# Two neighbouring ring slots summed by one set of VectorE instructions, in a hybrid decoder layer

## The chip, the cores and the metric

One core of a Trainium2 chip runs the whole layer as one program. The metric is the device time of that program in microseconds (us); three runs of the kernel before were timed.

## What is computed

One decoder layer on 512 tokens of width 2048, all in float32: an input projection, two token mixers (stick-breaking attention and a gated recurrence), a gated merge, an output projection, and a feed-forward block. The change touches only the up projection of the feed-forward block:

```python
up = rmsnorm(h, g_ffn) @ w_up                 # 2048 -> 2 * 5632
up = causal_depthwise_conv(up, conv_w, conv_b)
gate, val = jnp.split(up, 2, axis=-1)
h = h + (jax.nn.silu(gate) * val) @ w_down    # 5632 -> 2048
```

## The kernel before

**Products in three parts.** Every float32 operand is split into a high part (a copy with fewer bits, made by ScalarE) and a low part (raw minus high, made by VectorE). TensorE does three products for each: high by high, high by low, low by high.

**Seven products for eight.** The up projection multiplies 2x2 blocks of 128x128 weights by 2x2 blocks of activations with seven products (`PRODUCTS`), in the Strassen-Winograd way. A weight slot therefore holds seven blocks of 128 columns: `S4, A12, A22, A11, S1, S3, S2`. Four come from memory; S1 and S3 are sums over two of them, S2 is a sum over S1 and A11, and S4 over A12 and S2. The block in place S4 arrives holding A21.

**The feed-forward stage** is a list of 528 slots, `TABLE`, written out in the program. A group of it has eight "up" slots (one for each pair of 128 rows of the contraction, `kp` 0 to 7, for one tile `f` of 44), followed by "down" slots: none after the first two tiles, two after each of tiles 2 to 5, four after each later one. TensorE does 21 matmuls of 256 columns in an up slot (L2122 to L2124), 12 of 512 columns in a down slot (L2157 to L2159). So a group takes 10 slots for f = 2 to 5 and 12 slots from f = 6 on.

**The ring.** Slot n uses place n % 6 of a ring of six (`w4_raw`, `w4_lo`, `w4_hi`). The low part lies over the raw one; a place takes 7 KB a partition. Places 0 and 1, 2 and 3, 4 and 5 lie next to each other in memory. For slot n:

- SP issues the load (L441) when TensorE has done slot n - 6: `sp_.wait_ge(slot_done, ...)` at L509.
- VectorE makes the block sums of an up slot, `sums(n)` at L1633: three instructions, L1641 (two blocks, 256 columns), L1646 and L1648 (one block each). The second and the third wait by semaphore for the one before.
- ScalarE makes the high part, `hi_slot(n)` at L929 (instruction L937), which for an up slot waits for the count of sums.
- VectorE makes the low part, `lo_slot(n)` at L1650 (instruction L1655), which waits for the high part.
- TensorE waits for the count of low parts in `up_slot(n)` at L2117.

The first 24 slots (`NPRE`) come with their sums made beforehand by DMA; `sums` leaves them out (`summed`). That leaves 328 up slots for which VectorE makes them.

**The order on each engine is written out by hand**, slot by slot, in a function `position(n)` for ScalarE (L1000) and one for VectorE (L1747):

```python
def position(n):        # VectorE
    sums(n + 3)
    lo_slot(n + 2)
    ...                 # then one piece of the conv, combine, normalise, ... work
```

So at position n the queue of VectorE holds sums of slot n + 3, then the low part of slot n + 2, then one of: `combine` (L1685 to L1690), `take_up` (L1697, L1701), `normalise` (L1710, L1713), `conv_tap` (L1725), `product` (L1738), `s_low` (L1744). ScalarE's position n begins with the high part of slot n + 3; behind it come conv terms, SiLU and `take_down` (L996), which copies a finished down bank to a stage buffer. GpSimd then issues a DMA that adds that buffer to the output in memory (L640).

Of the kernel before, what the change touches and what calls it, by code (L numbers as in the profile page):

```python
# [24 lines left out]
ALU = mybir.AluOpType  # L25
ACT = mybir.ActivationFunctionType

P = 128
# [41 lines left out]
RING = 6  # L70
SC = 4 * P
WC = 7 * P
# [39 lines left out]
UPS = [sum(t[0] == "up" for t in TABLE[NPRE:n]) for n in range(SLOTS + 1)]  # L112
# [6 lines left out]
S4, A12, A22, A11, S1, S3, S2 = range(7)  # L119
# [38 lines left out]
def build_program(nc, x_t, wstream, wgates, wslots, wfirst, params, out_t):  # L158
# [7 lines left out]
    def sb(name, cols, at, dt=F32):  # L166
        return nc.alloc_sbuf_tensor_at(name, [P, cols], dt, offset=base + at)
# [70 lines left out]

    K = 1024
    ring_at = [0, 7 * K, 14 * K, 21 * K, R1 + 46 * K, R1 + 53 * K]  # L240
    w4_raw = [sb(f"w4_raw{j}", WC, a) for j, a in enumerate(ring_at)]
    w4_lo = [sb(f"w4_lo{j}", WC, a, F32R) for j, a in enumerate(ring_at)]
    w4_hi = [sb(f"w4_hi{j}", WC, a + 4 * WC, F32R) for j, a in enumerate(ring_at)]
    VC = 7 * HALF
# [89 lines left out]
    w4_in = [sem(f"w4_in{j}") for j in range(RING)]  # L334
    w4_step, w4_sums, w4_hi_ready, w4_ready, slot_done = (
        sem("w4_step"), sem("w4_sums"), sem("w4_hi_ready"), sem("w4_ready"), sem("slot_done"))
# [19 lines left out]
    def place(n):  # L356

        return n, n % RING, n // RING + 1

    def entry(n):  # L360
        return TABLE[n]

    def summed(n):

        return n < NPRE

    def is_up(n):
        return entry(n)[0] == "up"

    def exists(n):  # L370
        return n < SLOTS
# [52 lines left out]
    def blocks(t, j, n=1):  # L424
        return t[:, j * P:(j + n) * P]
# [4 lines left out]
    with nc.Block() as block:  # L430
# [221 lines left out]
        def _(act):  # L652
# [276 lines left out]
            def hi_slot(n):  # L929
                if exists(n):  # L930
                    at_, ring, loads = place(n)
                    if is_up(n) and not summed(n):
                        act.wait_ge(w4_sums, UPS[n] + 1)
                    else:
                        act.wait_ge(w4_in[ring], loads * 16)
                    width = WC if is_up(n) else SC
                    act.activation(w4_hi[ring][:, 0:width], w4_raw[ring][:, 0:width], ACT.Copy).then_inc(w4_hi_ready, 1)  # L937
# [10 lines left out]
            act.wait_ge(unit_done, WSLOTS + START4 - 2)  # L948
            hi_kp(5)
            hi_slot(0)  # L950
            hi_kp(6)
            hi_slot(1)
            tile3(KT - 2)
            hi_slot(2)


# [116 lines left out]
        def _(dve):  # L1073
# [558 lines left out]

            def sums(n):  # L1633

                if not exists(n) or not is_up(n) or summed(n):
                    return
                at_, ring, loads = place(n)
                u = UPS[n]
                w = w4_raw[ring]
                dve.wait_ge(w4_in[ring], loads * 16)  # L1640
                dve.tensor_tensor(blocks(w, S1, 2).rearrange("p (a c) -> p a c", a=2),  # L1641
                                  blocks(w, 0).unsqueeze(1).broadcast_to((P, 2, P)),
                                  blocks(w, A22, 2).rearrange("p (a c) -> p a c", a=2),
                                  ALU.add).then_inc(w4_step, 1)
                dve.wait_ge(w4_step, u * 2 + 1)
                dve.tensor_tensor(blocks(w, S2), blocks(w, S1), blocks(w, A11), ALU.add).then_inc(w4_step, 1)  # L1646
                dve.wait_ge(w4_step, u * 2 + 2)
                dve.tensor_tensor(blocks(w, S4), blocks(w, A12), blocks(w, S2), ALU.add).then_inc(w4_sums, 1)  # L1648

            def lo_slot(n):  # L1650
                if exists(n):
# [15 lines left out]
            split_ahead(START3, KP - 1, 4, 0)  # L1667
            split_ahead(START3, KP - 1, 4, 1)
            sums(0)
            lo_kp(5)  # L1670
            t_sums(6)
            sums(1)
            lo_slot(0)
            lo_kp(6)
            tile3(KT - 2)
            sums(2)
            lo_slot(1)

# [590 lines left out]
```

## Time and profile before

| | |
|---|---|
| Median of 3 runs | 2807.22 us (2806.18 to 2808.89) |
| Span of the profiled execution | 2806.6 us |
| TensorE busy with matmuls | 2798.6 us of it |
| VectorE busy | 2087.2 us |
| ScalarE busy | 1248.4 us |
| GpSimd busy | 428.6 us |
| Feed-forward stage | from about 1438 us to the end |

The profiled execution is one run of the program; its span, from its first to its last instruction, lies 0.6 us under the median of the timed runs. Busy time of one engine can lie beside that of another, and matmuls overlap each other, so the mean time of one matmul is longer than the distance between two starts. In a timeline each row has its start and its duration in us, the engine, the line, the operation and the tiles; what stands in brackets is idle time in front of it and what ended it.

### The profile page before, as it was taken

How to read it: one execution, taken by the hardware profiler on the slowest of the kernel's cores; microseconds unless marked ns; L12 is line 12 of the kernel's file. 1: busy time of each engine (PE TensorE's matmuls, PEld its weight loads, DVE VectorE, ACT ScalarE, POOL GpSimd, SP SyncE). 2: the span in 40 equal slices, each digit the busy share in tenths (PEclk: the TensorE clock that was granted, in tenths of full speed). 3: DMA queues.
4: the chain of work that ended last, by engine and by line, in shares of the span. 5: the costliest groups of instructions: out<-in, count | busy, mean ns of one | idle time of the engine just before them, and what ended most of it. 6: DMA issues, size and time to landing. Idle time of an engine off the chain costs nothing.

```text
span 2806.6 us, 45334 instructions
## 1 busy us (share of the span) xinstructions
PE 2798.6 (100%) x16930; PEld 2513.6 (90%) x16930; DVE 2087.2 (74%) x3913; ACT 1248.4 (44%) x1701; POOL 428.6 (15%) x579
## 2 busy tenths in 40 slices
PE   9999999999999999999999999999999999999999
PEld 7788888888889999888899999999999999999998
DVE  7776677677777777444468987888788878887884
ACT  5444434433334334323355544444444444444543
POOL 1022154324400000001000111111111101110112
PEclk9999999999999999999999999999999999999999
DMA  5363586666534555444455655555555555565557
GB/s 177 137 184 94 176 193 132 177 186 128 113 115 157 175 168 176 147 134 150 142 170 145 142 136 136 134 138 137 137 133 139 136 135 136 136 137 137 136 137 165
DMA packets 187463, 411.24 MB, mean 147 GB/s; under 512 B 22288, under 2 KB 50320, under 8 KB 186128
## 3 DMA queue, kind: packets, MB, share of 16 engines
q1 hardware_dynamic: 120240, 283.90, 31.8%
q0 software_dynamic: 67040, 124.82, 23.7%
q8 instruction: 125, 2.05, 0.3%
q14 instruction: 58, 0.48, 0.0%
HBM read 347.81 MB, written 112.72 MB: 164 GB/s over the span
## 4 chain that ended last, share of the span: by engine, by line
PE 98%; DVE 1%; ACT 0%; DMA 0%; issue 0%; SPq 0%; DVEq 0%
PE bank L1852 12%; PE bank L1854 12%; PE bank L1853 12%; PE bank L2122 11%; PE bank L2124 11%; PE bank L2123 11%; PE bank L2157 6%; PE bank L2158 6%; PE bank L2159 6%; PE bank L2078 3%; PE bank L2079 3%; PE bank L2080 3%; PE bank L1926 1%; PE bank L1960 1%; PE bank L1971 0%; PE bank L1916 0%
## 5 line engine op out<-in xcount | busy, mean ns | idle before, releaser
L2122 PE MATMUL bank<-v_hi,w_hi 128*128 128x256 f32 x2464 | 697.6, 283 | 0.0
L2124 PE MATMUL bank<-v_hi,w_lo 128*128 128x256 f32 x2464 | 697.3, 283 | 0.0
L2123 PE MATMUL bank<-v_lo,w_hi 128*128 128x256 f32 x2464 | 697.3, 283 | 0.0
L937 ACT ACTIVATE w_hi<-w_raw 128x896 fp32r<-128x896 f32 (+1 forms) x528 | 444.9, 846 | 555.1 <-DVE w_raw L1648 384.4
L1655 DVE TENSOR_TENSOR w_lo<-w_raw,w_hi 128x896 fp32r<-128x896 f32 (+1 forms) x528 | 500.2, 953 | 126.9 <-ACT w_hi L937 126.0
L2122 PEld LDWEIGHTS bank<-v_hi,w_hi 128*128 128x128 f32 x2464 | 472.9, 192 | 2.0 <-issue 0.2
L2123 PEld LDWEIGHTS bank<-v_lo,w_hi 128*128 128x128 f32 x2464 | 472.9, 192 | 1.9 <-issue 0.2
L2124 PEld LDWEIGHTS bank<-v_hi,w_lo 128*128 128x128 f32 x2464 | 472.9, 192 | 0.0
L1852 PE MATMUL bank<-u_hi,w_hi 128*128 128x512 f32 x1000 | 396.2, 396 | 0.2 <-DVE w_lo L1078 0.2
L1854 PE MATMUL bank<-u_hi,w_lo 128*128 128x512 f32 x1000 | 390.5, 391 | 0.0
L1853 PE MATMUL bank<-u_lo,w_hi 128*128 128x512 f32 x1000 | 389.8, 390 | 0.0
L1078 DVE TENSOR_TENSOR w_lo<-w_raw,w_hi 128x1024 fp32r<-128x1024 f32 x189 | 230.5, 1223 | 133.5 <-ACT w_hi L658 131.4
L640 POOL DMA_DIRECT2D out_t<-stage x168 | 142.7, 851 | 1182.5 <-ACT stage L996 1059.7
L2157 PE MATMUL bank<-s_hi,w_hi 128*128 128x512 f32 x698 | 272.1, 390 | 0.0
L2158 PE MATMUL bank<-s_lo,w_hi 128*128 128x512 f32 x698 | 272.0, 390 | 0.0
L2159 PE MATMUL bank<-s_hi,w_lo 128*128 128x512 f32 x698 | 271.5, 389 | 0.0
L1854 PEld LDWEIGHTS bank<-u_hi,w_lo 128*128 128x128 f32 x1000 | 188.1, 188 | 40.1
L1852 PEld LDWEIGHTS bank<-u_hi,w_hi 128*128 128x128 f32 x1000 | 188.2, 188 | 38.4 <-DVE w_lo L1078 1.0
L1853 PEld LDWEIGHTS bank<-u_lo,w_hi 128*128 128x128 f32 x1000 | 188.4, 188 | 38.0 <-issue 0.2
L658 ACT ACTIVATE w_hi<-w_raw 128x1024 fp32r<-128x1024 f32 x189 | 197.4, 1049 | 19.9 <-DMA w_raw<-wstream 19.8
L2159 PEld LDWEIGHTS bank<-s_hi,w_lo 128*128 128x128 f32 x698 | 131.0, 188 | 27.6
L2157 PEld LDWEIGHTS bank<-s_hi,w_hi 128*128 128x128 f32 x698 | 131.2, 188 | 26.3 <-issue 0.2
(287 smaller groups left out, 4847.5 us busy)
## 6 DMA issues: line engine op xcount, KB each, us to landing
w_raw<-wslots SPq DMA_DIRECT2D x504, 256.0 KB, 2.7
w_raw<-wstream SPq DMA_DIRECT2D x189, 512.0 KB, 3.5
out_t<-stage POOLq DMA_DIRECT2D x168, 256.0 KB, 4.3
sums_scratch<-wfirst POOLq DMA_DIRECT2D x72, 448.0 KB, 5.7
g_raw<-sums_scratch SPq DMA_DIRECT2D x48, 448.0 KB, 3.2
g_raw<-wgates SPq DMA_DIRECT2D x48, 256.0 KB, 2.8
w_raw<-sums_scratch SPq DMA_DIRECT2D x24, 448.0 KB, 3.4
sums_scratch<-sums_scratch POOLq DMA_DIRECT2D x72, 128.0 KB, 4.7
```

Source lines behind the costliest of these rows:

```text
L937: act.activation(w4_hi[ring][:, 0:width], w4_raw[ring][:, 0:width], ACT.Copy).then_inc(w4_hi_ready, 1)
L1078: dve.tensor_tensor(w_lo[slot][:, :], w_raw[slot][:, :], w_hi[slot][:, :].bitcast(F32), ALU.subtract).then_inc(w_ready, 1)
L1655: dve.tensor_tensor(w4_lo[ring][:, 0:width], w4_raw[ring][:, 0:width], w4_hi[ring][:, 0:width].bitcast(F32), ALU.subtract).then_inc(w4_rea ...
L1852: nc.tensor.matmul(out, wh, hi, start=first, stop=False)
L1853: nc.tensor.matmul(out, wh, lo, start=False, stop=False)
L1854: return nc.tensor.matmul(out, wl, hi, start=False, stop=last)
L2122: nc.tensor.matmul(out, wh, xh, start=kp == 0 and half == 0, stop=False, skip_group_check=True)
L2123: nc.tensor.matmul(out, wh, xl_, start=False, stop=False, skip_group_check=True)
L2124: ins = nc.tensor.matmul(out, wl, xh, start=False, stop=kp == KP - 1, skip_group_check=True)
L2157: nc.tensor.matmul(out, wh, sh, start=first and f == fs[0], stop=False)
L2158: nc.tensor.matmul(out, wh, sl, start=False, stop=False)
L2159: ins = nc.tensor.matmul(out, wl, sh, start=False, stop=last and f == fs[-1])
```

## The change

`sums` now does nothing for an odd slot, and for an even slot n it makes the block sums of slots n and n + 1 together. Each of its three instructions covers the two places of the ring through one view (`w4_two`), with twice the columns: 512, 256 and 256. It waits for the loads of both slots. ScalarE's wait counts pairs instead of slots. The places in memory, the loads, the high and low parts and the products are as before. All groups of `TABLE` have even length, so a pair is always two up slots of one tile.

```diff
+    w4_two = [sb(f"w4_two{j}", 4 * WC, ring_at[2 * j]) for j in range(RING // 2)]
+    w4_raw = [w4_two[j // 2][:, 2 * WC * (j % 2):2 * WC * (j % 2) + WC] for j in range(RING)]
...
                     if is_up(n) and not summed(n):
-                        act.wait_ge(w4_sums, UPS[n] + 1)
+                        act.wait_ge(w4_sums, UPS[n] // 2 + 1)
...
-                if not exists(n) or not is_up(n) or summed(n):
+                if not exists(n) or not is_up(n) or summed(n) or n % 2:
                     return
                 at_, ring, loads = place(n)
-                u = UPS[n]
-                w = w4_raw[ring]
-                dve.wait_ge(w4_in[ring], loads * 16)
-                dve.tensor_tensor(blocks(w, S1, 2).rearrange("p (a c) -> p a c", a=2),
-                                  blocks(w, 0).unsqueeze(1).broadcast_to((P, 2, P)),
-                                  blocks(w, A22, 2).rearrange("p (a c) -> p a c", a=2),
-                                  ALU.add).then_inc(w4_step, 1)
+                u = UPS[n] // 2
+                w = w4_two[ring // 2][:, :].rearrange("p (s c) -> p s c", s=2)
+
+                def two(j):
+                    return w[:, :, j * P:(j + 1) * P]
+
+                def two_by_two(j):
+                    return w[:, :, j * P:(j + 2) * P].rearrange("p s (a c) -> p s a c", a=2)
+
+                for k in range(2):
+                    dve.wait_ge(w4_in[ring + k], loads * 16)
+                dve.tensor_tensor(two_by_two(S1), two(0).unsqueeze(2).broadcast_to((P, 2, 2, P)),
+                                  two_by_two(A22), ALU.add).then_inc(w4_step, 1)
                 dve.wait_ge(w4_step, u * 2 + 1)
-                dve.tensor_tensor(blocks(w, S2), blocks(w, S1), blocks(w, A11), ALU.add).then_inc(w4_step, 1)
+                dve.tensor_tensor(two(S2), two(S1), two(A11), ALU.add).then_inc(w4_step, 1)
                 dve.wait_ge(w4_step, u * 2 + 2)
-                dve.tensor_tensor(blocks(w, S4), blocks(w, A12), blocks(w, S2), ALU.add).then_inc(w4_sums, 1)
+                dve.tensor_tensor(two(S4), two(A12), two(S2), ALU.add).then_inc(w4_sums, 1)
```

## Rows read from the trace of the kernel before

**Rows 1.** The page: busy time of each engine, and the chain by engine.
```profile
PE 2798.6 (100%) x16930; PEld 2513.6 (90%) x16930; DVE 2087.2 (74%) x3913; ACT 1248.4 (44%) x1701; POOL 428.6 (15%) x579
...
PE 98%; DVE 1%; ACT 0%; DMA 0%; issue 0%; SPq 0%; DVEq 0%
```

**Rows 2.** Windows: stretch, its length, busy us of each engine, clock, DMA share, GB/s.
```profile
1480.00:1600.00 120.00, 120.00 (x915) 115.99 (x914) 109.07 (x205) 62.27 (x87) 13.61 (x16) 1.00 0.60 142
1600.00:2750.00 1150.00, 1150.00 (x7998) 1079.78 (x7997) 941.38 (x1814) 557.36 (x778) 125.66 (x148) 1.00 0.58 136
1503.00:1528.60 25.60, 25.60 (x193) 24.64 (x192) 24.50 (x48) 13.85 (x20) 3.44 (x4) 1.00 0.64 144
```

**Rows 3.** Groups by shape, VectorE, 1600 to 2600 us: busy us, mean ns, idle before.
```profile
L1655 DVE TENSOR_TENSOR w_lo<-w_raw,w_hi 128x896 fp32r<-128x896 f32 x257 | 279.0, 1086 | 0.6
L1641 DVE TENSOR_TENSOR w_raw<-w_raw 128x256 f32<-128x256 f32 x258 | 107.9, 418 | 0.0
L1655 DVE TENSOR_TENSOR w_lo<-w_raw,w_hi 128x512 fp32r<-128x512 f32 x129 | 86.8, 687 | 89.4 <-ACT w_hi L937 89.2
L1646 DVE TENSOR_TENSOR w_raw<-w_raw 128x128 f32<-128x128 f32 x258 | 75.4, 292 | 8.8
```

**Rows 4.** Timeline, VectorE, at 2004 us: L1688 waits for L1685, L1690 not for L1688.
```profile
2004.39 0.42 DVE L1685 TENSOR_TENSOR u_sum<-bank,g_sum 128x256 f32<-128x256 f32 x1 [2.10 <-ACT g_sum L966]
2004.85 0.42 DVE L1688 TENSOR_TENSOR v_sum<-u_sum,bank 128x256 f32<-128x256 f32 x1
2005.19 0.42 DVE L1690 SCALAR_TENSOR_TENSOR g_sum<-bank,u_sum 128x256 f32<-128x256 f32 x1
```

**Rows 5.** Timeline of a later group: slot 229's load, slot 227's low part and first matmul.
```profile
2015.02 0.33 SPq L441 DMA_DIRECT2D w_raw<-wslots  x1
...
2017.12 1.08 DVE L1655 TENSOR_TENSOR w_lo<-w_raw,w_hi 128x896 fp32r<-128x896 f32 x1
...
2022.23 0.28 PE L2122 MATMUL bank<-v_hi,w_hi 128*128 128x256 f32 x1
```

**Rows 6.** Loads L441 from 1600 to 2750 us: issue to landing.
```profile
DMA to landing us min/median/max: 2.4/2.7/5.1
```

**Rows 7.** DMA issues: slot 229's load (2015.02 us), then slot 167's (1854.28 us).
```profile
w_raw<-wslots SPq DMA_DIRECT2D x1, 256.0 KB, 3.3
...
w_raw<-wslots SPq DMA_DIRECT2D x1, 256.0 KB, 4.0
```

**Rows 8.** Timeline, group f = 3: slot 33's load is issued, slot 31 begins.
```profile
1508.48 0.33 SPq L441 DMA_DIRECT2D w_raw<-wslots  x1
...
1515.57 0.28 PE L2122 MATMUL bank<-v_hi,w_hi 128*128 128x256 f32 x1
```

**Rows 9.** Timeline, group f = 4: output DMAs, slot 43's load, slot 41's low part and start.
```profile
1532.09 0.84 POOL L640 DMA_DIRECT2D out_t<-stage  x1 [12.82 <-ACT stage L996]
1533.15 0.84 POOL L640 DMA_DIRECT2D out_t<-stage  x1 [0.21 <-issue]
...
1533.97 0.33 SPq L441 DMA_DIRECT2D w_raw<-wslots  x1
...
1539.23 1.08 DVE L1655 TENSOR_TENSOR w_lo<-w_raw,w_hi 128x896 fp32r<-128x896 f32 x1
...
1541.19 0.28 PE L2122 MATMUL bank<-v_hi,w_hi 128*128 128x256 f32 x1
```

**Rows 10.** DMA issues: loads of slots 33, 43, 53, 63, in this order.
```profile
w_raw<-wslots SPq DMA_DIRECT2D x1, 256.0 KB, 6.2
...
w_raw<-wslots SPq DMA_DIRECT2D x1, 256.0 KB, 5.7
...
w_raw<-wslots SPq DMA_DIRECT2D x1, 256.0 KB, 5.1
...
w_raw<-wslots SPq DMA_DIRECT2D x1, 256.0 KB, 5.5
```

**Rows 11.** Timeline, GpSimd, the group of rows 5: its second output DMA.
```profile
2012.60 0.85 POOL L640 DMA_DIRECT2D out_t<-stage  x1 [3.40 <-ACT stage L996]
```

More of the change, by code:

```diff
@@ L240, in build_program @@
     ring_at = [0, 7 * K, 14 * K, 21 * K, R1 + 46 * K, R1 + 53 * K]
-    w4_raw = [sb(f"w4_raw{j}", WC, a) for j, a in enumerate(ring_at)]
+    w4_two = [sb(f"w4_two{j}", 4 * WC, ring_at[2 * j]) for j in range(RING // 2)]
+    w4_raw = [w4_two[j // 2][:, 2 * WC * (j % 2):2 * WC * (j % 2) + WC] for j in range(RING)]
     w4_lo = [sb(f"w4_lo{j}", WC, a, F32R) for j, a in enumerate(ring_at)]
```

## The prediction, on record before the change was run

> **What bounds the kernel now.** I read the page first. TensorE is busy all the time, and the chain that ended last is 98% TensorE [rows 1]. Its 1% of VectorE could be worth up to 28 us, so I asked where it lies: the windows of the feed-forward stage show TensorE busy for 120.00 of 120 us and for 1150.00 of 1150 us, at full granted clock [rows 2]. So the VectorE pieces of the chain lie in the attention stage, which the change doesn't touch. In the stage that it does touch, TensorE never waits. VectorE is the second busiest there: 941.4 of 1150 us, and in the 10-slot groups 24.5 of 25.6 us [rows 2]. That is close to full, but VectorE is always ahead: the low part of slot 227 begins at 2017.12 and takes 1.08, so it is ready at 2018.20, and TensorE begins that slot at 2022.23, 4.0 us later [rows 5]. In group f = 4 the low part of slot 41 is ready at 1539.23 + 1.08 = 1540.31 and wanted at 1541.19, only 0.9 us later [rows 9]. What the reader is to see: nothing can be won from a stage whose bound never waits, and the question is only whether 0.9 to 4 us of lead survive.
>
> **The change, part by part.**
>
> *Fewer instructions.* 328 slots had three instructions each, of 418, 292 and 292 ns [rows 3]. Now 164 pairs have three of 512, 256 and 256 columns. For 512 columns I take 687 ns (the 512-column low part), for 256 columns 418 ns [rows 3]. An instruction that waits for the one before starts 0.46 us after it where the duration is 0.42, one that doesn't wait 0.34 us after it [rows 4]: so a wait makes the distance the duration plus about 0.03, no wait makes it the duration less 0.08. Before, a slot took (0.418 + 0.03) + (0.292 + 0.03) + (0.292 - 0.08) = 0.98 us of the queue, a pair 1.96. After: (0.687 + 0.03) + (0.418 + 0.03) + (0.418 - 0.08) = 1.50 us. Saved: 0.46 us a pair, 75 us of VectorE's time in all. All of it lies beside TensorE's work and is worth nothing while that never waits. The patterns now have one dimension more, with a step of 7 KB between slots. No row shows such a pattern. The bounds are 0 extra (cost goes by the number of columns, as in the rows) and, as an upper end, three single-slot sets not merged at all, 1.96 us; I take 0, since L1641 already has a repeated operand and two dimensions and has the price of L1685, which has neither [rows 3, 4].
>
> The Trainium skill, VectorE: DVE Perf Modes, section "The DRAIN you can't avoid", says that chained instructions pay the same with or without a semaphore between them. Rows 4 show 0.46 against 0.34 us, so the trace does not agree. By the rule all distances would be 0.08 under the durations and a pair would save 0.23 instead of 0.46 us; neither reaches TensorE.
>
> *A later wait.* Sums of slot n - 1 (even) stand at VectorE's position n - 4 and now also want the load of slot n. That load was wanted one position later before. It is issued when slot n - 6 is done, one slot (2.5 us) after the load of n - 1. Behind the waiting instruction, on VectorE's in-order queue, stand the low part of slot n - 2 and the conv work; behind the sums, on ScalarE, the high parts of n - 1 and n and the copies of down banks. The first one to be late is the low part of slot n - 2, since TensorE wants it first. From landing to its end: 0.05 us to start, 1.50 of sums, 1.09 of low part [rows 3], together 2.65 us. Its high part is older and is there.
>
> *The budget.* For a load n of the last pairs of a group, the low part must be there when slot n - 2 begins. Slot 229's load is issued at 2015.02 and slot 227 begins at 2022.23: 7.21 us, less 2.65 gives 4.56 us in which the load may land without a stall [rows 5]. It landed in 3.3 us [rows 7]. Over the later groups the loads take 2.4 to 5.1 us [rows 6]. I asked for the landing of each one: of the 144 second partners of the 36 groups f = 7 to 42 none took more than 4.0 (slot 167) [rows 7]; the 5.1 belongs to a load of a down slot, which no sum waits for. So these groups don't stall; their lead falls from 4.0 to about 4.56 - 3.3 = 1.3 us.
>
> *Where the budget is broken.* In groups f = 3 to 6 the load of the last partner (slots 33, 43, 53, 63) takes 6.2, 5.7, 5.1 and 5.5 us [rows 10]. The reason is seen in group 4: two output DMAs go out at 1532.09 and 1533.15, and the load follows at 1533.97 [rows 9]. The budgets are 1515.57 - 1508.48 - 2.65 = 4.44 us for slot 33 [rows 8] and 1541.19 - 1533.97 - 2.65 = 4.57 us for slot 43 [rows 9]; slots 53 and 63 have the same distances (7.22 and 7.09 us), so 4.57 and 4.44. Stalls: 6.2 - 4.44 = 1.8; 5.7 - 4.57 = 1.1; 5.1 - 4.57 = 0.5; 5.5 - 4.44 = 1.1. Sum 4.5 us. After such a stall the conv work is late too, but the following position has no sums and gives the time back: slot 42 is wanted one slot, some 2.5 us, after slot 41, and between the two low parts VectorE has one low part (1.09) and one piece of conv work of 512 columns (about 0.7, as the 512-column row). What is unsure is the landing itself. The copies of down banks stand behind the high part that waits for the pair, and behind conv terms, so the output DMAs go out some 0.4 to 0.8 us later than now, nearer to or on top of the load. Lower bound: the load slips ahead of the second of them and takes the 3.3 to 4.0 us of rows 7, stall 0. Upper bound: each takes the longest of the four, 6.2 us, stall 1.6 to 1.8 each, 6.8 us. I keep 4.5, the landings as they are.
>
> *ScalarE's counts, memory places, loads:* same instructions as before, nothing added.
>
> Sum: 2806.6 + 4.5 = 2811.1 us of span; the median of the runs lies 0.6 above the profiled span, so 2811.7, or +0.16%.
>
> **Rivals.** A difference of 0.2% (5.6 us) is about what a measurement of this kernel can tell from none; it puts "slower" above 2812.8 us and "faster" under 2801.6.
>
> 1. *All hidden.* The output DMAs, moved by ScalarE's delay, no longer hit the load of the last partner, or it lands within 4.4 us. For it: most loads land in 2.7 us [rows 6], so one that gets ahead of both output DMAs is safe by 1.7. Against: the four landings of rows 10 all lie over the budget, and the move is smaller than a slot. Time 2807.2. Chance 0.25.
>
> 2. *The later groups stall too* (the other side). In the group of rows 5 the second output DMA goes out at 2012.60 [rows 11], 2.4 us ahead of the load of slot 229. With ScalarE's copy standing behind the pair's high part it moves about 1 us towards that load. If the load then lands later than 4.56 us, every group stalls. The point from which it decides is 4.7 us: 0.15 us for each of 36 groups is 5 us, and with the early groups that is +10. At 5.1 us (the longest of rows 6) it is 0.54 x 36 = 19, and 2831 with the early groups. Against: 4.0 is the longest seen among the partners [rows 7]. Chance 0.15. The Trainium skill, DMA: Bandwidth & Descriptors, section "Issuing engines are not separate DMA queues", says that transfers from all issuing engines run on the same 16 DMA engines and interleave; rows 10 agree, with 5.1 to 6.2 us against the median of 2.7 [rows 6], and by it the load is delayed whichever of the two goes first.
>
> 3. *The wider pattern costs more.* At 1.96 us a pair instead of 1.50 the budgets shrink by 0.46: early groups 4.5 + 4 x 0.46 = 6.3 us, later ones hold (4.10 against 4.0). Time 2813.6. That is also the case in which the change saves VectorE nothing. Chance 0.10.
>
> 4. *Faster.* VectorE's 75 us come back. It would need TensorE to wait for VectorE in this stage or matmuls to run closer together; both windows show it busy throughout [rows 2]. Time 2732 if all came back, and any time under 2801.6 counts. Chance 0.03.
>
> 5. *Likeliest:* stalls in groups f = 3 to 6 only, 2809 to 2814 us, 2811.7 the middle. Chance 0.47.
>
> **Numbers.** Within 0.2%: all of rival 1 and seven tenths of the likeliest, 0.25 + 0.33 = 0.58. Slower: three tenths of it and rivals 2 and 3: 0.14 + 0.15 + 0.10 = 0.39. Faster 0.03. The range begins a little under rival 1, at 2806, and ends in the lower half of rival 2, at 2821; about 0.12 is left out.
>
> **What the changed profile would show.** VectorE busy about 79 us less (328 x 1.002 against 164 x 1.523 us of durations), near 2008 us. In the lines of `sums`, 164 instructions each at 0.69, 0.42 and 0.42 us. VectorE idle time at the first of them ended by the load. TensorE idle for 0.5 to 1.8 us at slots 31, 41, 51 and 61, its sum near 4.5 us, ended by the low part L1655 in which the load of two slots later is seen behind; nothing at the later groups. The prediction is wrong if TensorE idles at slots like 227, if the early loads land in under 4.4 us, or if the new instructions last longer than rows of their width.

## The result, and the profile after

| | before | after |
|---|---|---|
| Median | 2807.67 us (11 runs, 2806.18 to 2808.89) | 2813.91 us (11 runs, 2812.41 to 2817.07) |
| Span of the profiled execution | 2806.6 us | 2811.1 us |
| VectorE busy | 2087.2 us | 2028.2 us |

The ratio is 1.0024, with a 95% interval of 1.0016 to 1.0031: slower by 6.2 us in the medians, 4.5 in the two profiled executions. The profiled run of the changed kernel took 2812.58 us, near the quick end of its runs.

The page of the changed kernel, its busy times and its chain by engine, against [rows 1]:

```profile
PE 2799.0 (100%) x16930; PEld 2513.1 (89%) x16930; DVE 2028.2 (72%) x3421; ACT 1228.8 (44%) x1701; POOL 427.9 (15%) x579
...
PE 95%; DVE 2%; issue 2%; DMA 1%; ACT 1%; SPq 0%; POOL 0%; DVEq 0%; POOLq 0%; ACTq 0%
```

VectorE has 492 instructions fewer and 59 us less to do, and the chain now passes more often through it, ScalarE and the DMAs. Windows of the feed-forward stage, against [rows 2], columns as there:

```profile
1480.00:1600.00 120.00, 116.26 (x873) 111.24 (x872) 99.77 (x153) 59.26 (x86) 13.62 (x16) 1.00 0.58 136
1600.00:2750.00 1150.00, 1149.56 (x7994) 1079.32 (x7994) 888.95 (x1371) 538.25 (x777) 125.70 (x148) 1.00 0.60 136
```

TensorE was busy for 120.00 and 1150.00 us there. It now lacks 3.74 us in the first 120 us of the stretch, which hold the first down slot (slot 24) and nearly all of the groups f = 3 to 6, and 0.44 in the 1150 us after them. The groups of VectorE by shape, against [rows 3]:

```profile
L1650 DVE TENSOR_TENSOR w_two<-w_two 128x512 f32<-128x512 f32 x128 | 88.2, 689 | 102.4 <-DMA w_two<-wslots 102.4
L1662 DVE TENSOR_TENSOR w_lo<-w_two,w_hi 128x512 fp32r<-128x512 f32 x130 | 87.0, 686 | 8.3 <-ACT w_hi L938 7.6
L1655 DVE TENSOR_TENSOR w_two<-w_two 128x256 f32<-128x256 f32 x128 | 54.4, 425 | 4.4
```

A 512-column instruction with the new pattern takes 689 ns, 256 columns take 425. And the idle time has moved: the sums stood ready when VectorE came to them (idle 0.0 in rows 3); now it stands still for 102.4 us in front of them, waiting for loads. Who waited for whom from 1480 to 1600 us (total us, times, longest):

```profile
PEld bank L2129 <- DVE w_lo L1662: 2.6, 5, 0.9
PEld bank L2164 <- issue: 2.3, 1, 2.3
PE bank L2164 <- DVE s_lo L1751: 2.2, 1, 2.2
PE bank L2129 <- DVE w_lo L1662: 1.4, 3, 0.7
```

PE and PEld rows tell of the same stalls twice. A matmul is drawn 0.28 us long while the next starts 0.12 after it, so a wait of up to 0.16 us doesn't show between matmuls; the weight load in front of a late matmul shows it. So I add up the PEld rows: 4.9 us here, and 0.6 for the rest of the stage (once, between 1900 and 2000 us), 5.5 in all.

**The largest stall is one that the prediction doesn't have.** Timeline of VectorE, ScalarE and TensorE at slot 24, the first down slot:

```profile
1494.05 0.69 DVE L1650 TENSOR_TENSOR w_two<-w_two 128x512 f32<-128x512 f32 x1 [4.58 <-DMA w_two<-wslots]
...
1495.69 0.95 ACT L938 ACTIVATE w_hi<-w_two 128x896 fp32r<-128x896 f32 x1 [6.34 <-DVE w_two L1655]
1496.55 0.61 ACT L988 ACTIVATE s_hi<-s_raw 128x512 fp32r<-128x512 f32 x1
...
1497.19 0.69 DVE L1751 TENSOR_TENSOR s_lo<-s_raw,s_hi 128x512 fp32r<-128x512 f32 x1 [0.93 <-ACT s_hi L988]
...
1498.14 0.47 PE L2164 MATMUL bank<-s_hi,w_hi 128*128 128x512 f32 x1 [2.17 <-DVE s_lo L1751]
```

Read upwards: TensorE waits for the low part of the activations of tile 1, that for their high part, which stands on ScalarE behind the high part of slot 26, which waits for the sums of the pair 26/27, and these stood still for 4.58 us until the load of slot 27 landed. Before, the same low part began at 1496.48 and the slot at 1497.43:

```profile
1496.48 0.69 DVE L1744 TENSOR_TENSOR s_lo<-s_raw,s_hi 128x512 fp32r<-128x512 f32 x1 [0.94 <-ACT s_hi L987]
...
1497.40 0.19 PEld L2157 LDWEIGHTS bank<-s_hi,w_hi 128*128 128x128 f32 x1 [0.17 <-issue]
1497.43 0.47 PE L2157 MATMUL bank<-s_hi,w_hi 128*128 128x512 f32 x1
```

From the end of the low part to the first matmul it is 0.26 us in both kernels (1497.17 to 1497.43, 1497.88 to 1498.14), and before, too, the weight load there stood still, for 0.17 us. So TensorE already waited for this low part before the change. It is the one wait that the rows of the stage show in that trace, and the place had no lead at all.

The starts of the low part lie only 0.7 us apart, and the stall grew by 2.2, since in its profiled execution the changed kernel came to slot 24 1.5 us earlier: the last matmul of slot 23 starts at 1495.69, before at 1497.16. Of that, 0.7 us were there at 92 us already. The other 0.8 came between there and the feed-forward stage, in work that the change doesn't touch, where TensorE ran for a time at its lower clock (1.2 GHz) in the kernel before alone. The same 3 us, before and after:

```profile
119.00:122.00 3.00, 3.00 (x8) 2.30 (x7) 2.70 (x17) 0.00 (x0) 0.00 (x0) 0.50 0.00 0
119.00:122.00 3.00, 3.00 (x15) 2.48 (x14) 2.66 (x17) 0.00 (x0) 0.00 (x0) 1.00 0.00 0
```

So the 4.5 us between the two spans understate what the stage lost. From the last matmul of slot 23 to the end it was 1309.4 us before and 1315.4 us after: 6.0 us longer, close to the 6.2 of the medians.

**The stall that was predicted is there, smaller.** The same at slot 31, whose low part stands behind the sums of 32/33 (VectorE, then TensorE), and the landing of slot 33's load:

```profile
1514.44 0.69 DVE L1650 TENSOR_TENSOR w_two<-w_two 128x512 f32<-128x512 f32 x1 [2.76 <-DMA w_two<-wslots]
1515.16 0.42 DVE L1653 TENSOR_TENSOR w_two<-w_two 128x256 f32<-128x256 f32 x1
1515.62 0.42 DVE L1655 TENSOR_TENSOR w_two<-w_two 128x256 f32<-128x256 f32 x1
1515.96 1.08 DVE L1662 TENSOR_TENSOR w_lo<-w_two,w_hi 128x896 fp32r<-128x896 f32 x1
...
1517.10 0.38 PE L2129 MATMUL bank<-v_hi,w_hi 128*128 128x256 f32 x1 [0.67 <-DVE w_lo L1662]
```
```profile
w_two<-wslots SPq DMA_DIRECT2D x1, 256.0 KB, 5.2
```

From the first sum to the end of the low part: 1517.04 - 1514.44 = 2.60 us, as worked out (2.65 with the start). The load took 5.2 us instead of 6.2 and the stall was 0.9 (PEld) instead of 1.8. At slot 61 it was 0.8 instead of 1.1, with a load of 5.5 us as before.

**At slots 41 and 51 there is none.** The loads of slots 43 and 53 took 4.2 and 2.9 us, under the budget of 4.57, where it had been 5.7 and 5.1 [rows 10]. The load of slot 43 now goes out between the two output DMAs, where it had followed both [rows 9]:

```profile
1535.22 0.84 POOL L641 DMA_DIRECT2D out_t<-stage  x1 [15.73 <-ACT stage L997]
...
1535.60 0.33 SPq L442 DMA_DIRECT2D w_two<-wslots  x1
1536.28 0.84 POOL L641 DMA_DIRECT2D out_t<-stage  x1 [0.21 <-issue]
```

So does that of slot 53. The load of slot 63 goes out between its two as well and yet took 5.5 us, so this place is not the whole reason.

**And a third kind**, in groups f = 4 to 6 two slots earlier, 0.2 to 0.4 us each. Timeline at slot 49, the three engines:

```profile
1561.36 0.60 ACT L997 ACTIVATE stage<-bank 128x512 f32<-128x512 f32 x1 [0.46 <-PE bank L2131]
1561.86 1.78 ACT L938 ACTIVATE w_hi<-w_two 128x896 fp32r<-128x896 f32 x2
...
1562.83 1.09 DVE L1662 TENSOR_TENSOR w_lo<-w_two,w_hi 128x896 fp32r<-128x896 f32 x1 [0.18 <-ACT w_hi L938]
...
1563.98 0.39 PE L2129 MATMUL bank<-v_hi,w_hi 128*128 128x256 f32 x1 [0.17 <-DVE w_lo L1662]
```

No load is late here. The copies of down banks come later on ScalarE, the high part of slot 49 stands behind them, and its low part is late by 0.2 us. No run moves these copies alone, so this reading rests on the order of the rows.

The one wait after 1600 us is at slot 179: the load of slot 181 took 5.0 us, more than the 4.56 of the budget and than any second partner of the later groups before.

### The profile page after: what moved, and what is told of

Read it like the earlier page. It is cut to its first block, busy times and chain, and to the rows that moved or that the text cites. A ratio compares the mean times of both kernels' runs of the same rounds, so it can differ in the third digit from the quotient of the medians.

```text
span 2811.1 us, 45006 instructions
## 1 busy us (share of the span) xinstructions
PE 2799.0 (100%) x16930; PEld 2513.1 (89%) x16930; DVE 2028.2 (72%) x3421; ACT 1228.8 (44%) x1701; POOL 427.9 (15%) x579
## 4 chain that ended last, share of the span: by engine, by line
PE 95%; DVE 2%; issue 2%; DMA 1%; ACT 1%; SPq 0%; POOL 0%; DVEq 0%; POOLq 0%; ACTq 0%
PE bank L1859 12%; PE bank L1861 12%; PE bank L1860 12%; PE bank L2129 10%; PE bank L2131 10%; PE bank L2130 10%; PE bank L2164 5%; PE bank L2165 5%; PE bank L2166 5%; PE bank L2085 3%; PE bank L2087 3%; PE bank L2086 3%; PE bank L1933 1%; PE bank L1967 1%; DMA out_t<-stage 1%
## 5 line engine op out<-in xcount | busy, mean ns | idle before, releaser
L938 ACT ACTIVATE w_hi<-w_two 128x896 fp32r<-128x896 f32 (+1 forms) x528 | 438.2, 841 | 570.9 <-DVE w_two L1655 414.4
L1662 DVE TENSOR_TENSOR w_lo<-w_two,w_hi 128x896 fp32r<-128x896 f32 (+1 forms) x528 | 496.5, 952 | 35.6 <-ACT w_hi L938 33.9
L1650 DVE TENSOR_TENSOR w_two<-w_two 128x512 f32<-128x512 f32 x164 | 113.0, 689 | 135.2 <-DMA w_two<-wslots 135.1
```

The costliest lines, as they stand in the source:

```text
L1662: dve.tensor_tensor(w4_lo[ring][:, 0:width], w4_raw[ring][:, 0:width], w4_hi[ring][:, 0:width].bitcast(F32), ALU.subtract).then_inc(w4_rea ...
```

## The experiments

Each kernel is set against the kernel before on the same chip; ratios have 95% intervals. Medians are of 11 runs, but of 8 for "low part first", 5 for "two sets at once" and 2 for "wait for a third load". "PEld waits" is the sum of those rows over the stage (1480 to 2740 us, in the last row to 2850); the kernel before has 0.2. "From slot 24 on" says by how much the profiled execution is longer than that of the kernel before from the last matmul of slot 23 to its end. It holds the short waits that stand in no row and what a lower clock costs, and leaves out what happens ahead of the stage.

| kernel | ratio | interval | median, us | its before | PEld waits, us | from slot 24 on, us |
|---|---|---|---|---|---|---|
| changed kernel | 1.0024 | 1.0016 to 1.0031 | 2813.91 | 2807.67 | 5.5 | 6.0 |
| slots 26, 27 one by one | 1.0016 | 1.0007 to 1.0025 | 2811.64 | 2807.13 | 5.2 | 5.2 |
| last pairs of f = 3 to 6 one by one | 1.0021 | 1.0012 to 1.0030 | 2813.68 | 2807.13 | 5.2 | 6.5 |
| slots 24 to 63 one by one | 1.0005 | 0.9996 to 1.0014 | 2808.82 | 2807.13 | 0.6 | 0.5 |
| before, the waits alone | 1.0019 | 1.0010 to 1.0028 | 2812.56 | 2807.13 | 2.9 | 4.2 |
| before, one wait | 1.0007 | 0.9998 to 1.0016 | 2809.20 | 2807.59 | 1.9 | 1.7 |
| before, two sets at once | 1.0052 | 1.0039 to 1.0066 | 2821.27 | 2807.59 | 11.3 | 13.1 |
| low part first | 1.0028 | 1.0017 to 1.0038 | 2815.01 | 2807.39 | 5.7 | 7.6 |
| low part first, 26/27 one by one | 1.0015 | 1.0006 to 1.0024 | 2811.20 | 2807.39 | 4.2 | 4.3 |
| 24 to 63 one by one, then low part first | 1.0001 | 0.9992 to 1.0010 | 2807.51 | 2807.59 | 0 | -0.2 |
| before, one instruction for three | 1.0000 | 0.9991 to 1.0009 | 2806.95 | 2807.39 | 0 | -0.2 |
| wait for a third load | 1.0360 | 1.0341 to 1.0378 | 2907.92 | 2807.39 | 94 | 101.6 |

The theory: the time is lost to the later wait, through what stands behind it in the in-order queues of VectorE and ScalarE, at the few places with little lead. The rival: the wider instructions themselves, or something spread over the whole stage, cost it.

**Slots 26 and 27 one by one.**

```diff
+ONE_BY_ONE = [26]
...
-                if not exists(n) or not is_up(n) or summed(n) or n % 2:
+                if not exists(n) or not is_up(n) or summed(n):
+                    return
+                alone = n - n % 2 in ONE_BY_ONE
+                if n % 2 and not alone:
                     return
...
```

A slot that is summed alone waits for its own load only and has the three instructions of before.

> The changed kernel, but slots 26 and 27 are summed one by one as before. The theory (the time is lost where work stands behind the later wait): the wait of 2.2 us at slot 24 goes, the other idle of TensorE stays (near 3 us): span near 2809, ratio 1.0016. Rival (the wider instructions themselves, or something spread over the whole stage, cost the time): no difference to the changed kernel, ratio 1.0024, span 2811.

The ratio is the expected one, 2.3 us less in the medians and 1.7 against each one's kernel before, though the intervals of the two ratios overlap and the rival's 1.0024 is inside. The profiled execution gained less: its span is 2811.5 us and not 2809, from slot 24 on it is 0.8 us shorter than the changed kernel. The stall at slot 24 is gone, and the others have grown, from 3.2 to 5.2 us and not "near 3". TensorE at slot 31, and the load behind it:

```profile
1516.76 0.39 PE L2144 MATMUL bank<-v_hi,w_hi 128*128 128x256 f32 x1 [1.59 <-DVE w_lo L1677]
```
```profile
w_two<-wslots SPq DMA_DIRECT2D x1, 256.0 KB, 6.1
```

With TensorE on time at slot 24, slot 33's load takes 6.1 us and the stall is 1.6 by the matmuls, 1.8 by the weight load: the prediction's own 6.2 and 1.8. The load goes out 1.7 us behind the first of the two output DMAs, as before (6.2 us); in the changed kernel it goes out 2.5 us behind it (1509.18 against 1506.67) and takes 5.2. That distance goes with the landing, but a stall at slot 24 alone doesn't make it: with one wait (below) it is 1.7 us again, and the load takes 6.0.

**The last pairs of f = 3 to 6 one by one** (the same edit, `ONE_BY_ONE` = 32, 42, 52, 62). These are the places where the prediction put all of its 4.5 us.

> The changed kernel, but the pairs 32/33, 42/43, 52/53 and 62/63, which the prediction named, are summed one by one. The prediction as it stood: 4.5 us less, ratio 1.0008. The reading of the changed kernel's trace: only the idle at slots 31 and 61 (0.8 us each) goes, that at slots 39, 49 and 59 (0.15 to 0.3) and the 2.2 at slot 24 stay: 1.5 us less, ratio 1.0019. Rival of wide instructions: 1.0024.

As good as nothing came back in the median, less than both figures; the prediction's 1.0008 is outside the interval, the 1.0019 of the trace's reading and the rival's 1.0024 are both inside, so this run doesn't tell those two apart. The profiled run shows the 2.4 us at slot 24, and new waits in place of the old:

```profile
PEld bank L2144 <- DVE a_gate L1723: 1.2, 1, 1.2
PE bank L2144 <- DVE a_gate L1723: 0.8, 1, 0.8
PEld bank L2144 <- DVE w_lo L1677: 0.5, 1, 0.5
PE bank L2144 <- DVE w_lo L1677: 0.3, 1, 0.3
```

These are rows from 1582 to 1600 us: TensorE waits for `take_up` (L1723), which frees its banks. In groups this full, what one place gains shows as lateness of the next.

A second thing hides the gain: behind the stall at slot 24 the granted clock fell to 1.2 GHz, and the slot's matmuls were about 1.7 us longer for it. In the changed kernel, whose stall there was as long, the same window has 1.00:

```profile
1500.00:1502.00 2.00, 2.00 (x6) 1.51 (x6) 1.97 (x5) 0.00 (x0) 0.00 (x0) 0.50 0.00 0
```

Without these 1.7 us the profiled run would be about 1.2 us shorter from slot 24 on than the changed kernel (an estimate from 6.5 and 6.0), near the 1.5 expected.

**Slots 24 to 63 one by one** (`ONE_BY_ONE` = the even numbers 24 to 62).

> The changed kernel, but all pairs from slot 24 to 63 are summed one by one, and the 144 pairs behind them two at a time as in the changed kernel. The theory: no idle of TensorE above 0.5 us in all, ratio 1.0000 to 1.0003, with seven eighths of the wide instructions in place. Rival of wide instructions: seven eighths of the loss stays, ratio 1.0021.

The expectation miscounts: of the twenty even slots four are down slots, so 148 of 164 wide sets are in place, not 144, and the rival would give 1.0022. The loss is 1.7 us in the medians and can't be told from none; 1.0005 is a little over the 1.0003 of the theory. TensorE is busy for 120.00 of 120 us in the early stretch, and waits once later, 0.6 us. The rival's figure lies outside the interval, by either count.

**The waits alone**, no wide instruction:

```diff
                 dve.wait_ge(w4_in[ring], loads * 16)
+                if n % 2 == 0:
+                    dve.wait_ge(w4_in[ring + 1], loads * 16)
```

> The kernel before with nothing but the later wait: sums of an even slot also wait for the load of the odd slot behind it; instructions, their widths and places in the queue as before. The theory: slot 24 waits for the low part of the activations 2.2 - 0.5 = 1.7 us (one set of sums, 0.98 us, stands in the chain in place of 1.50), and the early groups, whose VectorE is not relieved, lose 1 to 4 us: ratio 1.0010 to 1.0020. Rival of wide instructions: nothing lost, ratio 1.0000.

Slower by 5.4 us with the instructions of before: the rival's 1.0000 is out of the interval. The profiled run waits 1.9 us at slot 24 and 1.0 once in the early groups; the stage is 4.2 us longer, and the rest is many short waits of about 0.14 us that stand in no row. Of the same kind, **one wait** (`if n == 26:` in place of the condition):

> The kernel before with one semaphore wait more: the sums of slot 26 also wait for the load of slot 27. The theory of slot 24: that one wait costs 1.8 to 1.9 us, as in the kernel with all the later waits, ratio 1.0007, and the whole of it is seen at slot 24 in the wait for the low part of the activations. Rival: the trace's 2 us there are made up elsewhere, ratio 1.0000.

It waits for the low part of the activations at slot 24 and nowhere else, rows from 1480 to 1502 us:

```profile
PEld bank L2159 <- issue: 1.9, 1, 1.9
PE bank L2159 <- DVE s_lo L1746: 1.7, 1, 1.7
```

The medians differ by 1.6 us, and from slot 24 on the profiled run is 1.7 us longer: the wait of 1.9 less the 0.2 that the kernel before has there. The interval alone doesn't exclude none, the trace does.

**Two sets at once:** the waits and the places of the change, six instructions of the old widths.

```diff
             def sums(n):
+                if n % 2 == 0:
+                    one_slot(n)
+                    one_slot(n + 1)
+
+            def one_slot(n):
...
                 dve.wait_ge(w4_in[ring], loads * 16)
+                if n % 2 == 0:
+                    dve.wait_ge(w4_in[ring + 1], loads * 16)
...
```

> Placement and wait of the change without its wide instructions: at the even slot, six instructions of the old widths, for both slots, after both loads. The theory: 1.96 instead of 1.50 us between load and low part, so slot 24 waits 2.7 us, and the early groups, whose VectorE isn't relieved, lose more than in the changed kernel: 5 to 9 us in all, ratio 1.0025 to 1.0035. The difference to the changed kernel is what the wider instructions give back. Rival of wide instructions: 1.0000, since none is there.

It lost more than I expected, 13.7 us, with small waits in many places (19 for low parts, 8.6 us in all; ten of them after 1600 us). At slot 24 it waited 1.9 and not 2.7: here the sums are counted slot by slot, and ScalarE begins the high part of slot 26 when the first of the two sets is done. The changed kernel, which does the same sums in 1.50 instead of 1.96 us, loses 7.4 us less: given the later wait, wide instructions help.

**Low part first.**

```diff
             def position(n):
 
-                sums(n + 3)
                 lo_slot(n + 2)
+                sums(n + 3)
```

> The changed kernel, but at each position VectorE makes the low part of slot n + 2 ahead of the sums of slots n + 3 and n + 4, so that it no longer stands behind the later wait. The theory: the idle of TensorE ahead of up slots 31 to 61 goes (2 to 3 us); slot 24 waits for a low part of activations that still stands behind the sums and behind ScalarE's high part, and keeps its 2.2 us: ratio 1.0008 to 1.0013. Rival (wide instructions): 1.0022.

Wrong for the early groups: nothing gained, 5.7 us of waits. The rival's 1.0022 is inside the interval, so the time alone doesn't decide here. The profiled run again has a spell at 1.2 GHz behind the stall at slot 24 (granted clock 0.50 from 1500 to 1502 us), which makes up most of the distance between 5.7 us of waits and 7.6 us from slot 24 on. The low part of slot n - 2 no longer stands behind the load, but the sums are 1.1 us later, and the low part of the next slot now waits for ScalarE (VectorE's waits, 1502 to 1600 us):

```profile
DVE w_lo L1662 <- ACT w_hi L938: 10.8, 14, 1.9
DVE w_two L1650 <- DMA w_two<-wslots: 4.0, 3, 3.1
```

In the changed kernel the first of these was 0.2 us in that stretch, the second 12.4: one wait was traded for the other. In these groups, where VectorE had 1.1 us to spare of 25.6 before the change [rows 2], that didn't pay; in the later groups 70 us of waiting for ScalarE hurt nobody (TensorE 1150.00 of 1150 us).

**Both mendings:**

> Both mendings: the low part ahead of the sums, and slots 26 and 27 summed one by one. The theory: no idle of TensorE above 0.5 us, ratio 1.0000 to 1.0004, with 163 of 164 wide sets in place. Rival (wide instructions): 1.0022.

1.0015 and not 1.0004, for the same reason: the early groups keep 4.2 us of waits. The rival's 1.0022 is inside the interval here, so this run speaks for neither; the trace, with no wait after 1600 us and 163 wide sets, does for the theory.

**Slots 24 to 63 one by one, then pairs with the low part first:**

> Slots 24 to 63 summed one by one, as before; from there pairs, with the low part of slot n + 2 ahead of them. The theory: the early groups need their old order, the later ones have lead enough for the pair once the low part doesn't stand behind it: no idle of TensorE at all in the stage, ratio 1.0000 to 1.0004, with 144 of 164 wide sets in place. Rival (wide instructions): 1.0021.

Level with before, and TensorE without a gap, with 148 of 164 wide sets; the rival's 1.0021 is outside the interval:

```profile
1480.00:1600.00 120.00, 120.00 (x910) 115.87 (x909) 108.71 (x206) 62.15 (x88) 13.60 (x16) 1.00 0.60 141
1600.00:2750.00 1150.00, 1150.00 (x7997) 1079.85 (x7996) 894.90 (x1372) 536.07 (x777) 125.60 (x148) 1.00 0.59 136
```

VectorE is 46.5 us less busy than before in the second window, and the time is the same.

**One instruction for three.** The kernel before with one instruction of 384 columns in each slot instead of the three sums; it leaves out the sums S2 and S4 as the reference needs them.

```diff
-                dve.tensor_tensor(blocks(w, S1, 2)...)      # and the two behind it
+                dve.tensor_tensor(blocks(w, S1, 3).rearrange("p (a c) -> p a c", a=3),
+                                  blocks(w, 0).unsqueeze(1).broadcast_to((P, 3, P)),
+                                  blocks(w, A12, 3).rearrange("p (a c) -> p a c", a=3),
+                                  ALU.add).then_inc(w4_sums, 1)
```

> The kernel before, with one instruction of 384 columns a slot in place of the three sums (so the sums are not those of the reference): no later wait, and VectorE is relieved of 0.98 - 0.47 = 0.5 us a slot, 170 us in all, more than twice what the change saves. The theory (TensorE bounds the stage and waits for nothing): ratio 1.0000, within 0.0007. Rival (VectorE's time is worth something, and the change loses it again elsewhere): faster, down to 2640 us if all of it came back, and under 0.998 if a thirtieth did.

Nearly half of the time of the sums is gone (0.55 instead of 1.00 us a slot; VectorE 134 us less busy, not the 170 expected), and no time is won. So cheaper sums alone bring nothing here.

**A third load waited for** (the changed kernel, with a wait for the load of slot n + 2 behind the other two):

> The changed kernel, with the sums of a pair also waiting for the load of the slot behind it, which is issued one slot (2.52 us) later still. It doses the wait in all groups. The theory of the budget: 4.56 - 2.52 = 2.04 us for the landing, with loads of 2.6 us in three of four pairs and 3.8 in the last: 0.2 + 0.6 + 0.6 + 1.8 us a group, about 3 us, over some 40 groups 85 to 140 us, 2895 to 2950 us. If the budget is wrong (TensorE has more lead than it says): under 20 us.

100.5 us slower, inside what the budget gave. The waits of TensorE from 1480 to 2850 us:

```profile
PEld bank L2131 <- DVE w_lo L1664: 81.1, 83, 2.6
PE bank L2131 <- DVE w_lo L1664: 64.2, 82, 2.4
PEld bank L2166 <- issue: 9.2, 21, 4.6
PE bank L2166 <- DVE s_lo L1753: 4.4, 1, 4.4
PEld bank L2131 <- DVE a_gate L1710: 4.0, 3, 1.3
```

The three PEld rows are 94.3 of the 100.5 us. 2.52 us of extra wait a pair move every group over the edge on which the changed kernel stops short.

## Why the prediction was right, and where it was not

*Bound, right.* VectorE's saved time is worth nothing: one instruction in place of three gave 1.0000. But "TensorE never waits" was read from windows, in which a wait of 0.17 us doesn't show. It had one, at slot 24, just where the largest stall then came.

*Price of the sums, right.* 0.689, 0.425 and 0.425 us against 0.687, 0.418 and 0.418; no extra for the pattern (the 256-column ones take 7 ns more). VectorE was less busy by 59 us, though, and not by 79. That forecast added up durations, and of durations 328 x 1.002 - 164 x 1.539 = 76 us did go. But the page's busy time counts what overlaps once, and the last instruction of each set overlaps the next by 0.08 us: (1.002 - 0.08) x 328 - (1.539 - 0.08) x 164 = 63 us, near the 59.

*The later wait, right in kind.* The waits alone cost 1.0019; the chain from load to low part measured 2.60 us against 2.65; the budget of the later groups held but once (0.6 us of waits in 36 groups, where a load took 5.0 us, over the 4.56), and broke where a third load was waited for, within the 85 to 140 us expected.

*The places, half right.* The step that failed is "the first one to be late is the low part of slot n - 2, since TensorE wants it first". It is so within the groups, but at slot 24 the first to be late is the low part of the activations, two queues further on: 2.3 us (PEld) that no term of the sum held, at a place with no lead before. The prediction named the high parts of n - 1 and n behind the wait on ScalarE, and not what stands behind those.

*The size of the four terms.* 1.8 + 1.1 + 0.5 + 1.1 = 4.5 us were forecast; the profiled run has 2.6 in those groups, of which only 0.9 (slot 31) and 0.8 (slot 61) are at the places named. The landings moved. At slots 43 and 53 this was the prediction's own lower bound: the output DMAs went out later, the loads slipped ahead of the second one and landed in 4.2 and 2.9 us. The stall at slot 24 is not the cause, since without it they land in 3.2 and 3.1. At slot 33 it was 5.2 instead of 6.2, and there it is 6.1 and 1.8 without that stall.

*The total, in part luck.* The span of 2811.1 us was hit to the decimal because three errors met: terms of 4.5 us that measured 1.7 at their places, 3.8 us of stalls that no term held (slot 24, the third kind, slot 179), and 1.5 us that the profiled run of the kernel before lost ahead of slot 24 and that of the changed kernel did not. From slot 24 on the loss was 6.0 us and not 4.5. The median lies 2.2 us over the forecast of 2811.7, inside the range; the chance went more to "same" (0.58) than to "slower" (0.39), and with a ratio of 1.0024 the latter came, by a little. Undoing just the four named pairs gave nothing measurable back, which the forecast, taken by itself, could not have explained.

*Rivals.* All hidden: no. The later groups stalling: they did once, 0.6 us, by the mechanism named there. A costlier pattern: no, measured. Faster: no.

What stays open: runs of the changed kernel spread over 4.7 us, those of before over 2.7. Two things that differ between the profiled executions could do it: how long a load takes that meets output DMAs (2.8 to 6.2 us for slot 33, from kernel to kernel), and whether the clock falls behind the stall at slot 24 (it did with the last pairs one by one and with the low part first, about 1.7 us each, and did not in the changed kernel). Of the changed kernel's eleven runs the three with a mean granted clock of 1.000 have a median of 2812.6 us, the eight with 0.999 one of 2814.5; that fits, but no run varies the clock alone. For the waits alone the medians say 5.4 us, the profiled run 4.2 from slot 24 on; the rest is open, as are the 1.7 us of "24 to 63 one by one" against 0.5.

## What to carry to other kernels

Merging the work of two buffers into one instruction also merges their waits: the instruction starts when the later buffer is there, and everything behind it in that queue, and behind its consumer in the next queue, waits too. So list for each thing behind the merged instruction when it is wanted, through every in-order queue, and look at the fullest stretch and at the first of its kind (here the first down slot), not at a typical one. Ask the trace of before for the short waits that its windows hide: here the only one, 0.17 us, named the place of the largest stall. And on an engine that isn't the bound the saving is worth nothing: here level was the best outcome, and it took the old order in the 40 slots with little lead to get it.

## What the runs showed of the hardware

- A load of 256 KB that takes 2.7 us as a rule took 5.1 to 6.2 when it was issued 0.8 to 1.4 us behind the second of two adding DMAs of the same size from GpSimd's queue (0.8 in [rows 9]). For slot 33, how long it took went with the distance from the first of the two: 5.8 to 6.2 us at 1.7 (four kernels), 5.8 at 2.1, 4.5 to 5.2 at 2.4 to 2.9 (four kernels), 3.8 and 3.9 at about 4. Issued just ahead of both it took 2.8 (low part first, 26/27 one by one), so the prediction's remark that such a load is delayed whichever goes first is not borne out. Issued between the two it took 2.9 to 5.5 us in the changed kernel.
- A stall of TensorE under about 0.16 us doesn't show in its busy time, since matmuls of 256 columns are drawn 0.28 us long at 0.12 us from start to start. With six narrow instructions a pair, PE rows had 6.4 us of waits, PEld rows 11.3, and the median was 13.7 us longer. Waits of 0.14 us stand in neither; the distance from one fixed matmul to the end holds them all (13.1 us longer).
- A wait of TensorE of one length lowered its clock in one execution and not in another. Behind 2.7 us without a matmul at 115 to 119 us the granted clock was 0.50 (1.2 GHz) from 119 to 122 us in the kernel before and 1.00 (2.4 GHz) in the changed one; behind 2.2 to 2.3 us at slot 24 it was 0.50 from 1500 to 1502 us in one kernel and 1.00 in the other. The spell at slot 24 cost about 1.7 us.
- With a third load waited for, the clock was 0.97 in the stretch from 1480 to 1600 us, in which TensorE was busy for 106.17 of 120 us. It was at 0.50 from 1501.2 to 1503.2, at the end of a wait of 4.4 us and behind it, and fell once more soon after (0.66 in 1524 to 1529). In the 1150 us after them the mean still rounds to 1.00, with two short spells (0.66 in 2074 to 2079 and in 2671 to 2676 us).
